# Page groups of the sample's score stage: odd ones issued from ACT's DMA queue, even ones from SP's

## What is computed

```
kc = compress_blocks(k_cmp, cmp_pe[0], cmp_w1[0], cmp_w2[0])
vc = compress_blocks(v_cmp, cmp_pe[1], cmp_w1[1], cmp_w2[1])
...
s = jnp.einsum('btkgd,bnkd->bkgtn', qg, kc).astype(F32) * ATT_SCALE + head_bias(rel_bias, d_cmp)
...
s = jnp.einsum('bqkgd,bkqmd->bkgqm', q_b, kg).astype(F32) * ATT_SCALE + bias
```

## Time and profile before

| what | value |
| --- | --- |
| median of 3 runs | 2682.31 us |
| lowest and highest | 2681.46 and 2682.4 us |
| the profiled execution's own time | 2679.2 us |
| its span in the trace | 2677.4 us |
| mean granted clock of TensorE | 0.941 |
| PE busy | 2424.3 us, 91% |
| DVE busy | 1170.2 us, 44% |
| ACT busy | 500.7 us, 19% |
| DMA queue of SP (q1) | 253.65 MB |
| DMA queue of ACT (q10) | 18.35 MB |
| line 999's DMAs | 512 of 192 KB, median 3.3 us from issue to landing |

### The profile page before, as it was taken

One profiled execution on the slowest core, in us unless ns is written; L12 is line 12 of the kernel. 1 busy time (PEld: TensorE's weight loads), 2 busy tenths in 40 slices (PEclk: granted clock), 3 DMA queues, 4 the chain that ended last, 5 costly groups with the idle time before them and its releaser, 6 DMA issues. The chain is left out here.

```text
span 2677.4 us, 38154 instructions
## 1 busy us (share of the span) xinstructions
PE 2424.3 (91%) x13788; PEld 2041.5 (76%) x13788; DVE 1170.2 (44%) x2381; ACT 500.7 (19%) x1183; POOL 295.8 (11%) x322
## 2 busy tenths in 40 slices
PE   8996999699798999999989869986998989999997
PEld 6873999567597788888778659985667868888885
DVE  1933555445457544101048245554554575440012
ACT  1013111223421211000011221122242222110001
POOL 0600000000222011001015000000003221110010
PEclk9996999799899999999999979997999999999998
DMA  6214888244210222522042168852440103214310
GB/s 190 79 39 133 238 241 241 65 126 131 72 28 31 79 79 79 142 63 63 0 123 71 31 168 232 236 174 84 140 133 28 42 17 108 82 48 113 76 32 34
DMA packets 335879, 273.89 MB, mean 102 GB/s; under 512 B 53569, under 2 KB 331458, under 8 KB 335482
## 3 DMA queue, kind: packets, MB, share of 16 engines
q1 hardware_dynamic: 309288, 253.65, 33.4%
q10 hardware_dynamic: 26450, 18.35, 2.4%
HBM read 262.07 MB, written 18.17 MB: 105 GB/s over the span
## 5 line engine op out<-in xcount | busy, mean ns | idle before, releaser
L2643 PE MATMUL psum<-ff,HT 128*128 128x272 f32 x1536 | 353.3, 392 | 0.0
L447 PE MATMUL psum<-xT,ring 128*128 128x272 f32 x1408 | 327.7, 396 | 21.2 <-PEq L169 21.2
L2643 PEld LDWEIGHTS psum<-ff,HT 128*128 128x128 f32 x1536 | 291.8, 190 | 60.2
L447 PEld LDWEIGHTS psum<-xT,ring 128*128 128x128 f32 x1408 | 270.1, 192 | 77.9 <-issue 21.7
L1141 DVE STREAM_TRANSPOSE turned<-ring 128x1536 f32<-128x1536 f32 x128 | 227.4, 1778 | 190.0 <-DMA ring<-in_cache_nsa_kv 169.7
L1033 PE MATMUL psum<-turned,W 128*128 128x128 f32 x2048 | 262.2, 290 | 0.0
L1033 PEld LDWEIGHTS psum<-turned,W 128*128 128x128 f32 x2048 | 254.4, 206 | 0.0
L2489 PE MATMUL psum<-yT,HT 128*128 128x272 f32 x896 | 216.3, 399 | 0.0
L2489 PEld LDWEIGHTS psum<-yT,HT 128*128 128x128 f32 x896 | 173.2, 194 | 36.4
L1023 PE MATMUL psum<-yT,turned 128*128 (+1 forms) x1024 | 128.7, 281 | 49.1 <-DVE turned L1141 48.5
L1023 PEld LDWEIGHTS psum<-yT,turned 128*128 128x128 f32 x1024 | 124.6, 199 | 55.7 <-issue 46.8
(11 more groups left out here) (525 smaller groups left out, 3332.1 us busy)
## 6 DMA issues: line engine op xcount, KB each, us to landing
ring<-in_cache_nsa_kv SPq DMA_DIRECT2D x512, 192.0 KB, 3.3
ring<-in_w_up SPq DMA_DIRECT2D x32, 1024.0 KB, 5.6
ring<-in_cache_nsa_kv SPq DMA_DIRECT2D x384, 64.0 KB, 1.9
HT<-in_w_down SPq DMA_DIRECT2D x12, 2048.0 KB, 9.1
ring<-in_w_in SPq DMA_DIRECT2D x20, 1024.0 KB, 5.2
ring<-in_cache_nsa_kv ACTq DMA_DIRECT2D x128, 64.0 KB, 2.2
HT<-in_w_out SPq DMA_DIRECT2D x8, 1024.0 KB, 5.3
yT<-in_w_down SPq DMA_DIRECT2D x4, 2048.0 KB, 12.4
```

What stands on the lines that cost most here:

```text
L447: last = pe.matmul(psum[0:w.shape[1], 2 * (t % 3) + h, 0:HALF], w, S.xT[:, k, h * HALF:(h + 1) * HALF], start=(k == 0), stop=(k == KT - 1))
L2643: last = pe.matmul(out[h], down[t % 3][:, k, :], f[:, k, x], start=(k == 0), stop=(k == FT - 1))
```

## The change

A new function `load_group` holds what SP did for one group: the wait for the slot, the load of the page numbers (now 4 for each group) and 4 DMAs. SP calls it for groups 0, 2, 4 and 6 only. ACT calls it for groups 1, 3, 5 and 7, at fixed places of its own list: group 5 of sequence b before the silus, group 7 behind them, group 1 of sequence b+1 behind the copies of `vc`, group 3 of b+1 behind the copy of `wkt`. In sequence 0 ACT issues groups 1, 3, 5, 7 and group 1 of sequence 1 ahead of its first copy. The last sequence is taken out of ACT's loop and written out. Slots, semaphores, sizes and the work of PE, DVE and POOL stay.

```diff
--- before.py
+++ after.py
@@ -985,18 +985,20 @@
                     src = S.q_rows[HD * k + 32 * f:HD * k + 32 * f + 32, :].rearrange("p (b k r) -> p b k r", b=NB, k=KVH)[:, :, k, :]
                     copy(q_wide[32 * i:32 * i + 32, :, k, f, 8 * i:8 * i + 8], src).then_inc(sem, 1)
 
+            def load_group(eng, kind, b, g, first):
+
+                if not first or g >= slots:
+                    eng.wait_ge(s.turned, b * NG + (g - slots + 1))
+                numbers = page_numbers(S, kind, b, g * gp, gp)
+                for j, page in enumerate(numbers):
+                    src = layer(io.cache_nsa_kv, l)[ds(page, 1)].rearrange("a t c k d -> (a t) (c k d)")
+                    eng.dma_start(cache[:, g % slots, j, :], src[:, 0:3 * P].rearrange("(a e) n -> e a n", e=16)).then_inc(loaded[g % slots], 16)
+
             @block.sync
             def _(sp):
                 def sequence(b, first):
-                    for g in range(NG):
-                        if not first or g >= slots:
-                            sp.wait_ge(s.turned, b * NG + (g - slots + 1))
-                        if g % 2 == 0:
-                            numbers = page_numbers(S, mybir.EngineType.SP, b, g * gp, 2 * gp)
-                        for j in range(gp):
-                            page = numbers[(g % 2) * gp + j]
-                            src = layer(io.cache_nsa_kv, l)[ds(page, 1)].rearrange("a t c k d -> (a t) (c k d)")
-                            sp.dma_start(cache[:, g % slots, j, :], src[:, 0:3 * P].rearrange("(a e) n -> e a n", e=16)).then_inc(loaded[g % slots], 16)
+                    for g in range(0, NG, 2):
+                        load_group(sp, mybir.EngineType.SP, b, g, first)
                         if g == 0:
                             if not first:
                                 sp.wait_ge(s.w_turned, b)
@@ -1091,26 +1093,38 @@
 
             @block.scalar
             def _(act):
-                def compressed(b):
+                def compressed(b, after, after_first, following):
+                    if after is not None:
+                        load_group(act, mybir.EngineType.Activation, after, 5, after_first)
                     for n, c in enumerate((1, 0)):
                         act.wait_ge(s.added, b * 4 + (2 * n + 2))
                         act.activation(hid[:, c, :], hid[:, c, :], ACT.Silu, bias=S.pe_h[:, c:c + 1]).then_inc(s.swish, 1)
+                    if after is not None:
+                        load_group(act, mybir.EngineType.Activation, after, 7, after_first)
                     act.wait_ge(s.second, b + 1)
                     act.copy(kc[:, :], psum[:, 5, 0:NCB]).then_inc(s.kc_copied, 1)
                     for j in range(2):
                         m = P - j
                         act.copy(S.vc[0:m, j, ds(b, 1), :].rearrange("p a n -> p (a n)"),
                                  psum[0:m, 6, j * P:j * P + P]).then_inc(s.vc_copied, 1)
+                    if following is not None:
+                        load_group(act, mybir.EngineType.Activation, following, 1, False)
                     act.wait_ge(s.cmp_scored, b + 1)
                     for j in range(2):
                         m = P - j
                         act.copy(S.st_cmp[0:m, j, cols(b)], psum[0:m, 7, j * 16:j * 16 + 16]).then_inc(s.cmp_copied, 1)
 
-                def sequence(b, before):
+                def sequence(b, before, following):
                     if before is not None:
-                        compressed(before)
+                        compressed(before, b, False, following)
+                    else:
+                        for g in (1, 3, 5, 7):
+                            load_group(act, mybir.EngineType.Activation, b, g, True)
+                        load_group(act, mybir.EngineType.Activation, following, 1, False)
                     act.wait_ge(s.w_turned, b + 1)
                     act.copy(wkt, psum[:, 3, :]).then_inc(s.w_copied, 1)
+                    if following is not None:
+                        load_group(act, mybir.EngineType.Activation, following, 3, False)
                     act.wait_ge(s.scored, b + 1)
                     act.copy(S.st_sel[:, :, cols(b)], psum[:, 2, :].rearrange("p (t r) -> p t r", r=16)).then_inc(s.sc_copied, 1)
                     act.wait_ge(s.w_scored, b + 1)
@@ -1126,10 +1140,11 @@
                 for i in (1, 3):
                     for f in range(2):
                         spread(act.copy, i, f, s.q_act)
-                sequence(0, None)
-                with act.Fori(0, NB - 1) as i:
-                    sequence(i + 1, i)
-                compressed(NB - 1)
+                sequence(0, None, 1)
+                with act.Fori(0, NB - 2) as i:
+                    sequence(i + 1, i, i + 2)
+                sequence(NB - 1, NB - 2, None)
+                compressed(NB - 1, None, False, None)
 
             @block.vector
             def _(dve):
```

## The result

The changed kernel takes 2643.15 us (median of four runs, 2637.68 to 2644.01) beside 2682.35 us before: the ratio is 0.985, with a 95% interval of 0.9833 to 0.9867. The profiled execution, the slowest of the four, took 2644.01 us (span 2642.2).

The account below looks back on a forecast made before the run. SP's issue time set the 27.1 us period; after the change PE would bound at 25.6 us. Gains of 21.2 us (sequences 1 to 7) and 3.8 us (sequence 0), 25.0 us off 2682.3, gave 2657.3 us, range 2645 to 2673.

Parts of the forecast that it names:

- The bound before: Sample score stage before the change: SP's time to issue page DMAs sets the period, 27.11 us in layer 0.
- two signs: Page DMAs on SP: issues of even length (539 ns) and landings at a kept distance (3.3 us) spoke against full DMA engines.
- SP and ACT: Issuing queues: 11.8 us leave SP's 27 us list; ACT gains 13.1 us beside 4.55 us of copies, delaying no needed copy.
- Own work of PE: PE in one sequence: 26.83 us less the waits shown leaves 24.9 us, the new bound.
- Half-clock time: PE at 1.2 GHz: 0 to 1.2 us a sequence, taken as 0.6, plus 0.1 for waits, giving 25.6 us.
- half clock eats it: Rival: PE falls to 1.2 GHz as often or oftener, period 26.4 to 26.7 us, 2665 to 2676 us; chance 0.2.
- Sum of sequences 1 to 7: Stage in both layers: 179.2 us each against 187.8 and 191.8, a gain of 21.2 us.
- Sequence 0: Start of the stage: PE's idle 2.88 and 2.95 us go, group 1 comes 1 us later; gain 2 x 1.9 = 3.8 us.
- DMA share: DMA engines at a 25.6 us period: 256 GB/s, share 0.88 to 0.96, below 1, so no term.
- The rival of the DMA engines: DMA engines are the bound anyway, so a second queue only lengthens issues: 2680 to 2686 us; chance 0.08.
- Late ACT: Rival: group 5, queued behind ACT's last copy, lands late; period 28.3 us, 2695 us, slower; chance 0.06.
- SP then is never the bound: SP's list after the change: 16 page DMAs at 0.74 us, 11.8 us, go from a list 27 us long.

Follow-up runs that it names:

- e7: The kernel before with half of line 1033's matmuls left out, so PE's own work is shorter: 2678.28 us in a single run.
- e1: The kernel before with SP loading page numbers for each group (4 numbers), not every second group (8): ratio 1.0033, 2693.76 us beside 2683.84.
- e8: The changed kernel with half of line 1033's matmuls left out: 2634.44 us in a single run.
- e14: The changed kernel with one more PE wait, for ACT's second copy of `hb`, before the first score of sequences 1 to 7: ratio 0.993, 2662.8 us.
- e9: The changed kernel once more, unedited, run five times beside three other kernels on one chip: median 2638.0 us, ratio 0.9841.
- e13: The kernel of e8 with a third of each page's bytes also left out (128 KB a page): 2568.08 us in a single run.
- e4: The changed kernel with a load of page numbers for each page on both queues: ratio 0.9849, 2644.96 us.
- e2: The changed kernel, but ACT issues group 7 only and SP the other seven: ratio 0.9995, 2680.54 us beside 2683.84.
- e3: The changed kernel, but ACT issues groups 3 and 7 and SP the other six: ratio 0.9998, 2682.23 us beside 2683.84.

## Why the prediction was wrong, step by step

- **The bound before** ("SP's time to issue sets the period, not the slots and not the wires"): right, shown by e7 and e1. One of its two signs was weak. It took issues of even length as proof that the DMA engines were not full, but in e8, where they are the bound, an issue takes 540 ns at the median all the same. What differs there is the other sign, the time to landing: 6.1 us where it was 3.3.
- **SP and ACT** (a pace of 0.74 us; 13.1 us of ACT's time beside its copies): right. ACT issues four pages in 2.71 us, and its copies came in time.
- **Own work of PE, the step that failed** ("24.9 us of own work"). I subtracted the waits in brackets, 1.92 us, from a sequence of 26.83. PE's own work is 24.04 us: 10 of the 14 sequences after the change take that to 0.02 us. Set beside the pairs of the changed kernel (5.36, 6.23, 6.20, 6.25), those of before (5.96, 6.34, 6.85, 7.68) are longer by 0.60, 0.11, 0.65 and 1.43. The brackets account for 0.34, 0, 0.41 and 1.17 of that: three waits are 0.26, 0.24 and 0.26 us longer than shown, as in e14, and one of 0.11 us is not shown at all. That is the 0.87 us by which the floor was too high. Fourteen sequences make 12.2 us, which is most of the 14 us between forecast and result.
- **Half-clock time** ("I take the middle, 0.6, and 0.1 for waits"): sized too high, the second part of the same step. Sequences 1 to 7 took 170.8 us in layer 0 and 171.6 in layer 1, 24.40 and 24.52 each, so 0.4 us above 24.04 where I had 0.7: another 3.8 us. Half-clock time alone was 6.8 us in 14 sequences, which costs 0.24 us each where I had 0.6. I read the falls as bound to the work ahead of them ("one and the same", pair 3 with line 1050). That was misread: of the five falls in sequences 1 to 7 of layer 0 two come there (341.60, 368.90), and three (293.81, 321.12, 403.04) come 1.5 to 2.7 us after a first score that PE had waited 2.88, 0.63 and 1.55 us for. One of them, in the kernel before:

```profile
400.35 1.97 PE L1023 MATMUL psum<-yT,turned 128*128 x16 [1.55 <-DVE turned L1141]
402.15 5.44 PE L1033 MATMUL psum<-turned,W 128*128 128x128 f32 x32
```

The change removed most waits, and most falls with them; the rival "half clock eats it" fell with that.

- **Sum of sequences 1 to 7**: forecast 179.2 us for each layer, gain 21.2; measured gain 187.8 - 170.8 + 191.8 - 171.6 = 37.2.
- **Sequence 0** (2 x 1.9 us): both parts are seen, their sum is not. The idle 2.88 us at its end went, but group 1 was turned 2.25 us later and not 1. From SP's first DMA to the first score of sequence 1 it is 0.8 us less in layer 0 and 0.3 in layer 1. In the profiled execution of e9, the same kernel, it is 0.4 and 0.3 us more than before, so no gain at the start is shown.
- **DMA share** ("in proportion, a share of 0.88 to 0.96"): wrong. It is 0.98 to 1.11. Landings take 5.6 us in place of 3.3, and e8 with e13 puts the limit at about 24 us a sequence. The reserve that I took for small but present was almost nil; the forecast of the time did not hang on it, as PE stops at 24.04.
- **The rival of the DMA engines**, and with it the rule of the Trainium skill ("DMA: Bandwidth & Descriptors", section "Issuing engines are not separate DMA queues"): as a forecast for this change it failed, as the time to issue was the bound, 27.1 of 27.1 us. What the rule says of the mechanism holds: only the sequencer's time was saved, and the engines behind are shared and now full (a share of 0.98 to 1.11).
- **Late ACT** as a slower case: not seen. e4 gives the margin on ACT's side. That an in-order queue can eat the whole gain was shown by e2 and e3, but on SP and by a wait that I had not looked at: my reading "SP then is never the bound" left out what SP waits for once it is early.
- 37.2 + 1.1 us were gained in the stage and 35.2 in the profiled execution; 2.7 of the 3 us between them went in the other stages between layer 0's sample scores and layer 1's, where half-clock time was 110 us where it had been 108. Of the range: its lower end, 2645, took 24.9 us of own work as the floor, and so could not hold 2643.

## What to carry to other kernels

Where DMAs of one queue follow each other without a hole, at the length of their issue, and land at a constant and short distance, the queue's time is the bound here (the distance tells most: 3.3 us then, 6.1 us where the DMA engines bound); moving a quarter of them to an idle engine's queue can be enough. Then look at each wait in the relieved queue: the queue comes to it early, and what stands behind in order is held up, which with groups 3 and 7 cost all of the 39 us until one DMA was moved behind another group. For what the next engine can do, add its instructions in a stretch without waits rather than subtracting the waits shown.

## What the runs showed of the hardware that was not expected

- The trace shows a wait of PE 0.26 us shorter than it costs (0.78 shown, 1.04 paid in e14; 2.23 and 2.50 in e3).
- The time to issue a page DMA of 128 rows on SP did not follow its bytes: at the median 333 ns with rows of 512 bytes (line 1376), 540 with 1024 (e13) and 539 with 1536. The window's DMA of 256 KB took 450.
- A load of page numbers into registers takes about 270 ns for one (e4), 300 for four (e1) and about 530 for eight (kernel before; medians on SP).
- Pages of 192 KB in rows of 1536 bytes moved at 238 to 242 GB/s from one queue (kernel before) and at 256 to 280 from two (changed kernel), in stretches of 27 us in layer 0; the share of the 16 engines read 0.83 to 0.91 and 0.98 to 1.11. With the engines full (e8) they moved at 262 to 266 GB/s.
- Half clock came back with waits of 0.78 us in a stream of matmuls that was dense otherwise (e14): 27.3 us of it in 14 sequences, where the same kernel without the waits had 6.8.
